# Delta-rule input slabs in pairs by seven block products, inside the gated branch of a hybrid decoder trunk

## The reference

```python
def token_mixer(h, pos0, s_ret, s_gla, s_rwkv, s_shift, p, l):
    proj = (h @ p['w_in'][l]).astype(f32)
    p_ret, p_gla, p_rwkv, p_merge = split_cols(proj, (RET_PROJ, GLA_PROJ, RWKV_PROJ, MERGE_COLS))
    y_ret, sr = retention_branch(p_ret, ...)
    y_gla, sg = gla_branch(p_gla, ...)
    y_rw, sw, ss = rwkv7_branch(p_rwkv, ...)
...
def rwkv7_branch(p_rwkv, S0, prev0, mu, ...):
    prev = jnp.concatenate([prev0[:, None, :], p_rwkv[:, :-1, :]], axis=1)
    xm = p_rwkv + (prev - p_rwkv) * mu
```

## Time and profile before

| | before |
|---|---|
| median of 3 runs | 2505.91 us (2504.74 to 2508.6) |
| the profiled execution | 2506.55 us, span 2504.8 us |
| PE / DVE / ACT / POOL busy | 2448.9 / 1288.9 / 609.0 / 0.2 us |
| TensorE clock, mean of the span | 0.997 of full |
| gated branch, layer 0 | 231 to 384 us of the span |
| gated branch, layer 1 | 1222 to 1376 us of the span |

### The profile page before, as it was taken

The page is one execution under the profiler, slowest core; times in us unless marked ns, Lnnn a source line. Parts: engine busy times, 40 slices in busy tenths (PEclk is TensorE's granted clock), DMA queues, the critical chain, the costliest instruction groups (busy, mean ns, idle before and its releaser), DMA issues. The chain is left out here.

```text
span 2504.8 us, 103575 instructions
## 1 busy us (share of the span) xinstructions
PE 2448.9 (98%) x45930; PEld 2047.9 (82%) x45930; DVE 1288.9 (51%) x3327; ACT 609.0 (24%) x1798; POOL 0.2 (0%) x4
## 2 busy tenths in 40 slices
PE   9999999999999999999999999999999999999998
PEld 8987666666698999898766666679899999888986
DVE  7666666666686676756665666667311111111111
ACT  2233333433311100223333334321111111111111
POOL 0000000000000000000000000000000000000000
PEclk9999999999999999999999999999999999999999
DMA  6334432222243444333443222234899999999997
GB/s 249 111 136 162 150 134 88 83 83 79 90 163 121 159 173 134 133 116 137 154 161 125 84 77 83 83 105 152 321 357 391 385 364 386 393 388 397 407 391 284
DMA packets 146066, 500.42 MB, mean 200 GB/s; under 512 B 18785, under 2 KB 23521, under 8 KB 143361
## 3 DMA queue, kind: packets, MB, share of 16 engines
q1 hardware_dynamic: 145792, 496.44, 54.3%
HBM read 476.08 MB, written 20.29 MB: 198 GB/s over the span
## 5 line engine op out<-in xcount | busy, mean ns | idle before, releaser
L299 PE MATMUL psum<-hT,ring 128*64 128x144 f32 (+1 forms) x4568 | 457.1, 345 | 3.8 <-DVE hT L2419 1.7
L452 PE MATMUL psum<-work,ring 128*64 128x88 f32 (+1 forms) x11264 | 423.8, 235 | 10.3 <-issue 4.3
L452 PEld LDWEIGHTS psum<-work,ring 128*64 128x64 f32 x11264 | 411.6, 136 | 23.4 <-issue 20.5
L299 PEld LDWEIGHTS psum<-hT,ring 128*64 128x64 f32 x4568 | 291.7, 137 | 97.6 <-issue 12.2
L2959 DVE TENSOR_TENSOR work<-psum,work 128x88 f32<-128x88 f32 x176 | 43.9, 249 | 363.5 <-PE psum L452 363.3
L2659 PE MATMUL psum<-work,proj 128*64 128x88 f32 (+1 forms) x5632 | 212.1, 234 | 4.1 <-issue 2.7
L2659 PEld LDWEIGHTS psum<-work,proj 128*64 128x64 f32 x5632 | 205.1, 136 | 10.8 <-issue 9.6
L1765 ACT ACTIVATE work<-psum 128x256 f32<-128x256 f32 (+4 forms) x320 | 104.0, 362 | 349.7 <-PE psum L1676 84.8
L299 PE MATMUL psum<-y_ret,work 128*64 128x144 f32 x2400 | 157.9, 288 | 0.8 <-DVE y_ret L529 0.8
L299 PE MATMUL psum<-work 128*64 128x144 f32 (+4 forms) x2096 | 154.1, 282 | 4.3 <-DVE work L1256 3.6
L299 PEld LDWEIGHTS psum<-y_ret,work 128*64 128x64 f32 x2400 | 150.3, 138 | 1.2 <-issue 1.2
(11 more groups left out here) (514 smaller groups left out, 3725.9 us busy)
## 6 DMA issues: line engine op xcount, KB each, us to landing
ring<-w_ff_dram SPq DMA_DIRECT2D x424, 512.0 KB, 6.9
ring<-w_mix_dram SPq DMA_DIRECT2D x256, 512.0 KB, 4.4
proj<-w_ff_dram SPq DMA_DIRECT2D x128, 512.0 KB, 5.5
proj<-w_ff_dram SPq DMA_DIRECT2D x64, 384.0 KB, 5.7
work<-s_gla_dram SPq DMA_DIRECT2D x8, 1024.0 KB, 5.4
gla_s_out<-work SPq DMA_DIRECT2D x8, 1024.0 KB, 4.7
work<-s_ret_dram SPq DMA_DIRECT2D x8, 512.0 KB, 5.6
ret_s_out<-work SPq DMA_DIRECT2D x8, 512.0 KB, 3.0
```

The costliest lines, as they stand in the source:

```text
L299: last = nc.tensor.matmul(out[64 * c:64 * c + 64], weights[:, 64 * c:64 * c + 64], x, start=start, stop=stop)
L452: mm = nc.tensor.matmul(out[64 * c:64 * c + 64], ring[:, s, k, 64 * c:64 * c + 64], rhs[:, k0 + k, :], start=(k0 + k == 0), stop=(k0 + k = ...
```

## The change

`rwkv`'s 24 input slabs are made in 12 pairs by seven block products, as `retention` does it for the gated branch. PE's generator `row_products` yields 28 steps a pair; a step is two matmuls of 144 columns (4 records). Where `rw(4)` stood, `rw(7)` stands, and `rw(14)` for `rw(8)`, so a pair ends at the end of level 3, at the end of level 7, and at the end of the head. Two of a pair's four weight sums (s1, s3) are made by POOL (`outer_sums`), the other two (s2, s4) by DVE (`inner_sums`). POOL starts pair p when both slabs are there and pair p-2 is done. The sums lie in ring slots 6 and 7 (even pairs), or in `lora_w` and the first two slabs of `merged` (odd pairs); since that would overwrite the input sums, POOL copies those (2304 columns) to `work` once a layer. DVE combines with four instructions a pair (`take_x`, one; `take_y`, two; `take_z`, one), ACT copies one block (`take_first`), and `rw_row` now reads the combined result in SBUF. `new_states` is cut in two around `take_y`; rows and mixes of slabs 4 and 5 of a head move into the next head (behind the last head for head 3).

```diff
+        quad, copied = w(7, HALF), w(4, PAIRS_UP, HALF)
+        first_product = y_gla[:, KT - 1, 0:HALF]
...
+        def row_sums(p):
+            if p % 2 == 0:
+                return list(sum_tiles(ring_wsum, 4, 4))
+            return list(sum_tiles(rest_wsum, 3, 4)) + list(sum_tiles(last_wsum, 1, 4))
+        def fill_bank(p, fill):
+            return B[6 + (p + fill) % 2]
+        def slabs_of_pair(p):
+            return ring[:, 2 * p % 6], ring[:, 2 * p % 6 + 1]
...
+            def row_products():
+                for p in range(PAIRS):
+                    a1, a2 = slabs_of_pair(p)
+                    s1, s2, s3, s4 = row_sums(p)
+                    x, y, z = (fill_bank(p, n) for n in range(3))
+                    kept_sums = copied if p else xsum_kept
+                    xs = [[kept_sums[:, n, k, :] for k in range(PAIRS_UP)] for n in range(4)]
+                    pair_arrived(pe, p)
+                    if p:
+                        pe.wait_ge(sig("y_taken"), p)
+                    for k in range(PAIRS_UP):
+                        in_halves(x[:, 2 * HALF:3 * HALF], a1[:, k], inputs[k][:, 0:HALF], k == 0, k == 3)
+                        yield
...
+                    pe.wait_ge(sig("wsum"), 2 * p + 1)
+                    if p == 1:
+                        pe.wait_ge(sig("copied"), 1)
+                    for k in range(PAIRS_UP):
+                        last = in_halves(x[:, HALF:2 * HALF], s2[:, k], xs[1][k], k == 0, k == 3)
+                        if k == 3:
+                            last.then_inc(sig("first_ps"), 1)
+                        yield
+                    if p:
+                        pe.wait_ge(sig("taken"), p)
+                    pe.wait_ge(sig("outer_sum"), 2 * p + 2)
+                    for k in range(PAIRS_UP):
+                        in_halves(y[:, 0:HALF], s1[:, k], xs[0][k], k == 0, k == 3)
+                        yield
+                    for k in range(PAIRS_UP):
+                        last = in_halves(y[:, HALF:2 * HALF], s3[:, k], xs[2][k], k == 0, k == 3)
+                        if k == 3:
+                            last.then_inc(sig("middle_ps"), 1)
+                        yield
+                    pe.wait_ge(sig("wsum"), 2 * p + 2)
+                    pe.wait_ge(sig("u2"), p + 1)
+                    for k in range(PAIRS_UP):
+                        in_halves(z[:, 0:HALF], s4[:, k], inputs[k + 4][:, HALF:T], k == 0, k == 3)
+                        yield
+                    for k in range(PAIRS_UP):
+                        last = in_halves(z[:, HALF:2 * HALF], a2[:, k + 4], xs[3][k], k == 0, k == 3)
+                        if k == 3:
+                            last.then_inc(slab_done, 2)
+                        yield
+            blocks = row_products()
+            def rw(n):
+                for _ in range(n):
+                    next(blocks, None)
...
-                    rw(4, True)
+                    rw(7)
...
-                rw(4, True)
+                rw(7)
...
-                rw(4, True)
+                rw(7)
...
-                rw(8, True)
+                rw(14)
...
-            pe.wait_ge(sig("row"), GLA_H * 6 + 1)
+            pe.wait_ge(sig("y_taken"), PAIRS)
...
-                act.wait_ge(slab_done, i * 6 + (slabs_before(layer, S_RW) + j + 1))
+                act.wait_ge(sig("taken"), i * 3 + j // 2 + 1)
                 act.wait_ge(sig("mixed"), i * 6 + j + 1)
-                fill_row(row, kept, RW_ORDER[i][j], j % 2, B[6 + j % 2]).then_inc(sig("row"), 1)
+                c = j % 2
+                fill_row(row, kept, RW_ORDER[i][j], c, flat(quad[:, 2 * c:2 * c + 2, :])).then_inc(sig("row"), 1)
+            def take_first(p):
+                act.wait_ge(sig("first_ps"), p + 1)
+                if p:
+                    act.wait_ge(sig("u2"), p)
+                ac(first_product, fill_bank(p, 0)[:, 2 * HALF:3 * HALF], cp).then_inc(sig("first"), 1)
...
-            grant(act, sig("row"), by=2)
...
                 factors(i, 2)
                 decays(i)
                 if i:
+                    rw_row(i - 1, 4)
                     rw_row(i - 1, 5)
                 factors(i, 3)
+                take_first(3 * i)
                 if i:
                     rstd(i - 1)
                 factors(i, 4)
                 take_values(i)
-                rw_row(i, 0)
                 factors(i, 5)
                 take_keys(i)
                 factors(i, 6)
+                rw_row(i, 0)
                 rw_row(i, 1)
                 factors(i, 7)
+                take_first(3 * i + 1)
                 take_middle(i)
-                rw_row(i, 2)
                 if i + 1 < GLA_H:
                     factors(i + 1, 1)
+                rw_row(i, 2)
                 rw_row(i, 3)
                 take_output(i)
-                rw_row(i, 4)
+                take_first(3 * i + 2)
+            rw_row(GLA_H - 1, 4)
             rw_row(GLA_H - 1, 5)
             rstd(GLA_H - 1)
...
+            def outer_sums(p):
+                pair_arrived(pool, p)
+                if p >= 2:
+                    pool.wait_ge(slab_done, slabs_before(layer, S_RW) + 2 * p - 2)
+                s1, s2, s3, s4 = row_sums(p)
+                a1, a2 = slabs_of_pair(p)
+                nc.gpsimd.tensor_tensor(s1, a2[:, 0:4], a2[:, 4:8], ALU.add).then_inc(sig("outer_sum"), 1)
+                nc.gpsimd.tensor_tensor(s3, a1[:, 0:4], a2[:, 0:4], ALU.subtract).then_inc(sig("outer_sum"), 1)
+            pool.wait_ge(retained("y"), RET_H // 2 + 1)
+            outer_sums(0)
+            pool.wait_ge(retained("evac"), 6 + RET_H // 2 * 6)
+            nc.gpsimd.tensor_copy(copied, xsum_kept).then_inc(sig("copied"), 1)
+            for p in range(1, PAIRS):
+                outer_sums(p)
...
-                dve.wait_ge(sig("row"), i * 6 + j + 3)
+                dve.wait_ge(sig("row"), i * 6 + j + 1)
...
+            def inner_sums(p):
+                s1, s2, s3, s4 = row_sums(p)
+                a1, a2 = slabs_of_pair(p)
+                dve.wait_ge(sig("outer_sum"), 2 * p + 2)
+                tt(s2, s1, a1[:, 0:4], ALU.subtract).then_inc(sig("wsum"), 1)
+                dve.wait_ge(sig("wsum"), 2 * p + 1)
+                if p == 1:
+                    dve.wait_ge(sig("copied"), 1)
+                tt(s4, a1[:, 4:8], s2, ALU.subtract).then_inc(sig("wsum"), 1)
...
+            def take_x(p):
+                if p:
+                    dve.wait_ge(sig("row"), 2 * p)
+                dve.wait_ge(sig("first"), p + 1)
+                tt(quad[:, 0:5:4, :], two(fill_bank(p, 0)), rep(first_product, 1, 2), ALU.add).then_inc(sig("u2"), 1)
+            def take_y(p):
+                dve.wait_ge(sig("u2"), p + 1)
+                dve.wait_ge(sig("middle_ps"), p + 1)
+                tt(quad[:, 5:7, :], two(fill_bank(p, 1)), rep(quad[:, 4, :], 1, 2), ALU.add).then_inc(sig("u34"), 1)
+                dve.wait_ge(sig("u34"), p + 1)
+                tt(quad[:, 3, :], fill_bank(p, 1)[:, 0:HALF], quad[:, 6, :], ALU.add).then_inc(sig("y_taken"), 1)
+            def take_z(p):
+                dve.wait_ge(slab_done, slabs_before(layer, S_RW) + 2 * p + 2)
+                tt(quad[:, 1:3, :], two(fill_bank(p, 2)), quad[:, 5:7, :], ALU.add).then_inc(sig("taken"), 1)
...
-                for b in range(NB):
+                for b in sequences:
...
+            inner_sums(0)
             for i in range(GLA_H):
+                p = 3 * i
...
-                    if L == 0 and i:
-                        rw_mix(i - 1, 5)
+                    if L == 0:
+                        if i:
+                            rw_mix(i - 1, 4)
                     if L == 1:
                         scale_keys(i)
-                    if L == 2 and i:
-                        norm(i - 1)
+                        take_x(p)
+                    if L == 2:
+                        if i:
+                            rw_mix(i - 1, 5)
+                            norm(i - 1)
+                        take_y(p)
                     if L == 3:
+                        take_z(p)
+                        inner_sums(p + 1)
+                    if L == 4:
                         rw_mix(i, 0)
                     if L == 5:
+                        take_x(p + 1)
                         rw_mix(i, 1)
                     if L == 6:
                         sequence_keys(i)
+                        take_y(p + 1)
+                    if L == 7:
+                        take_z(p + 1)
+                        inner_sums(p + 2)
                 if i + 1 < GLA_H:
                     distance(i + 1, 1)
                 final_state(i)
@@ -1343,9 +1494,15 @@
                 if i + 1 < GLA_H:
                     level_keys(i + 1, 1)
                     distance_to_end(i + 1)
+                take_x(p + 2)
                 rw_mix(i, 3)
-                new_states(i)
-                rw_mix(i, 4)
+                new_states(i, range(4))
+                take_y(p + 2)
+                new_states(i, range(4, NB))
```

(4 more changed lines are left out.)

21 lines of the change are left out of this document (17 added, 4 removed).

## The result

The changed kernel takes 2544.97 us (median of 4 runs, 2543.62 to 2658.68), the kernel before in the same session 2505.32 us. The ratio is 1.0155, 95% interval 1.0138 to 1.0173: slower by 1.6%, some 39 us.

What follows compares the result with a forecast made beforehand. PE bounded the kernel before; afterwards a DVE loop through `take` of level 7, lengthened by POOL's sums, would. 2506.55 + 7.6 (loop and ends) + 24 (POOL) = 2538 us, 2537 as median; range 2490 to 2562 us.

Steps and rivals of the forecast that it cites:

- the likeliest case: Branch heads: DVE waits for POOL part of the time, 2520 to 2560 us; chance 0.50.
- PE's saving: Products of a head: 336 records, 20.6 us, replace six slabs, 23.6 us; PE saves 3.0 us a head.
- DVE's load: DVE's queue in a head: occupied time goes from 24.8 to 33.4 us, against PE's 33.7.
- The loop: From `take` of level 7 to the next: 6.9 + 0.7 + 28.7 + 1.6 = 37.9 us, 1.2 us more a head.
- the loop alone: Rival for the branch: POOL costs DVE nothing, 2514 us, spanning 2499 to 2516 us; chance 0.24.
- The end of the branch: Shift-row stores to the next phase's first product: two fills, `take_z` and late DVE add 1.8 us a layer.
- The saving of PE behind the last loop: From the last loop's end to the last product: PE saves 0.6 us.
- POOL beside DVE: POOL's sums at pair ends hold up DVE: 3.2 us a head, 2.4 in the first, 24 us for both layers.
- The signs named beforehand: Second head: PE brackets of 3 us or more released by DVE, 39 to 42 us long, longer DVE rows beside POOL.
- its sign of a wrong loop: DVE idle over 2 us a head for anything but `take_x` of the third pair and ACT's exponentials.
- PE stays the bound: Rival for the heads: DVE's loop is under 33.7 us, total 2484 us, half of it 2495 us; chance 0.17.
- Full blocking in every sum: Rival: every POOL sum blocks DVE for its whole length, 7.2 us a head, 58 us, total 2572 us; chance 0.09.

Runs made afterwards that it cites:

- sums early, all queues in line: All four sums on DVE, every queue reordered, first pair's sums ahead of `level_keys`, against the kernel before: 2509.38 us, ratio 1.0015.
- fills: Changed kernel with POOL filling the two sum areas three times each with a constant instead of summing: 2878.66 us, total unusable; second head 37.56 us.
- the kernel with the new order and the shorter mix: All four sums on DVE, PE making 12 steps ahead of `output(i, 0)`, mix cut to two DVE instructions: 2541.42 us, ratio 1.0148 to the kernel before.

## Why the prediction was right

**The time.** 2537 us were predicted, 2545 measured, and the likeliest case, that DVE waits for POOL part of the time, is the one that the runs show.

**PE's saving.** 3.0 us a head were to leave PE with 33.7 us. The best head that was seen (sums early, all queues in line) has PE busy for 34.6 us, so the saving is about 2.1 us. In that head the 336 records of products take 21.6 us, 0.0644 us each, where the step took 0.0613 us from a long row of one kind; PE's other work takes 12.95 us in both kernels. It didn't matter here, since PE wasn't the bound.

**DVE's load.** 33.4 us occupied were predicted. Without POOL's sums the head is 37.55 us with 4.4 us of DVE's waits in it: 33.1 us.

**The loop.** 37.9 us a head were predicted for the loop alone, 37.55 measured; +3.8 us a layer, +3.4 measured (157.2 less 153.8 in layer 0); 2514 us for this rival, 2513.23 measured. The stretch from the `take` of level 7 to `take_x`, 7.6 us predicted (with 0.2 us in it for the hand-over, for which there was no row), is 300.88 - 293.21 = 7.7 us in the run without POOL's sums. DVE's other stands are 2.6 us, 0.9 for ACT's exponentials and 1.7 of mixes for ACT's rows; 0.96 us of them lie inside that stretch and cost nothing, so 1.6 us lie on the loop, as much as predicted, though the wait for rows has the larger part. The loop came out 0.35 us too long because DVE's work on it was put too high, 28.7 us against 37.55 - 7.7 - 1.6 = 28.2.

**The end of the branch.** +1.8 us were predicted from the last square sum to the next phase; it is 6.6 us instead of 5.7, +0.8, with 0.8 us of stand ahead of the square sum, so +1.6 in all. The saving of PE behind the last loop was put at 0.6 us; by the prediction's own figures two slabs less 28 steps are 2 x 3.94 - 6.86 = 1.0 us. The first head without POOL's sums is 37.0 us, 0.8 shorter than before (-1.0 predicted).

**POOL beside DVE** is the term that was mis-sized: 24 us against 31.6. The length of a sum was right (1.27 us and 1.24 from start to start, 1.2 predicted), and so was the reasoning that the two sums behind pair 3i+1 are absorbed, which the run with the moved sums shows by itself. Of the other four I counted two thirds, a share that no row gave; three quarters landed, 3.7 us a head instead of 3.2. Over three loops that is 1.5 us a layer too little. The first head was worse: 41.6 against 37.0 us, 4.6 instead of 2.4. The copy of 2304 columns, priced at nothing because DVE waits there, has a part in it. Without POOL's sums the copy is there too, but it runs from 232.86 to 234.96 us, inside DVE's stand for ACT; POOL's first two sums push it behind that stand. Timeline of the changed kernel, first head:

```profile
234.58 2.11 POOL L1320 COPY work<-merged 128x2304 f32<-128x2304 f32 x1
235.51 1.49 DVE L1357 TENSOR_TENSOR work<-proj,work 128x288 f32<-128x288 f32 x1 [2.05 <-ACT work L1223]
...
236.93 1.51 DVE L1358 TENSOR_TENSOR work<-proj,work 128x288 f32<-128x288 f32 x1
...
238.37 1.75 DVE L1403 TENSOR_TENSOR ring<-ring 128x512 f32<-128x512 f32 x1
...
238.50 1.12 PE L299 MATMUL psum<-work 128*64 128x128 f32 x8 [4.12 <-DVE work L1358]
```

`level_keys` (L1357, L1358) beside that copy and the next POOL sum take 1.49 and 1.51 us instead of 0.45, and PE stands 4.1 us for them. DVE's wait for ACT ended while the copy still ran, and the cover ended with it. From L1357 to the start of the second inner sum DVE needs 4.6 us here and 1.6 without POOL's sums; by the rows, about 1 of these 3 us is the copy and 2 are the sums of the second pair. The other 1.5 us of the first head come with the later pairs.

On the mechanism the Trainium skill, "SBUF — State Buffer", section "Who interferes with whom", says that a DVE instruction with two SBUF inputs contends with a GpSimd instruction that reads SBUF, not with one that only writes it. By that rule, the traces agree in both halves: 0.69 us become 1.58 and 1.65 beside a sum, and stay 0.68 and 0.69 beside fills. The section also calls this an exclusive lock, so that one blocks until the other is done. The traces agree in part: six sums of 1.24 us are 7.4 us a head, and DVE's rows grew by 5.6. Of the difference, 0.8 us are the starts of the three pairs of sums (at 273.64, 290.03 and 302.48 us), when DVE stands or runs rows that read PSUM; the other 1.0 us is open.

**The signs named beforehand.** PE's brackets released by DVE sum to 4.2 us in the second head (at least 3 named), the head is 41.3 us (39 to 42), DVE's waits for PE at `new_states` are gone, DVE's rows beside POOL are longer, and the spacing of POOL's sums is 1.2 us. DVE stands for ACT alone, 1.7 us of it for rows, which the prediction had not named; its sign of a wrong loop was over 2 us.

**What the rivals were worth.** "The loop alone" is what happens without POOL's sums. "PE stays the bound" came near only in the rewritten order (PE busy for 34.6 of 35.9 us), and gave back at the ends what it won. Full blocking in every sum would be 58 us; 31.6 were measured, as DVE's rows grow by 5.6 us a head and not by 7.2, and 1.8 us of these fall into a stand.

## What to carry to other kernels

Before work goes from a full DVE queue to POOL, ask what POOL reads and what DVE runs meanwhile: beside DVE instructions with two SBUF operands a POOL sum cost the kernel 0.66 us, and the same sum on DVE 0.43 us. Count occupied time of an in-order queue, not its busy share of the kernel; DVE at 51% had 11.9 us a head to give, not half of 36.7. And saved PE time is only there if every queue that feeds it is put in a new order with it; each single move gave the gain to the next wait.

## What was not expected of the hardware

The wait of one engine for the other's SBUF reads stands inside its row in the trace, without a bracket: DVE's busy time of 1400.2 us contains it. It shows only when the mean of one form is compared between kernels.

TensorE's clock fell inside the branch, too. Behind PE's 2.49 us stand in the second head of the changed kernel the mean granted clock is 0.60 over the next four microseconds, between the lower of its two levels (1.2 GHz, 0.5) and the full one (2.4 GHz) (windows of all engines; clock, DMA share and GB/s are the last three columns):

```profile
284.00:288.00 4.00, 3.65 (x36) 2.73 (x38) 3.79 (x12) 1.40 (x4) 0.00 (x0) 0.60 0.50 193
288.00:292.00 4.00, 4.00 (x61) 3.63 (x59) 3.75 (x7) 1.07 (x4) 1.97 (x2) 0.97 0.30 73
```

The same products, from that stand to the group behind L1152, take 5.90 us there and 4.35 us without POOL's sums, where the stand was 0.98 us and the clock stayed at 1.00. It cost nothing in this head, as DVE never waits for PE in it: from that stand to `take_x` at 299.08 us DVE stands for ACT alone, at most 0.2 us at a time. Where the others wait for PE it does cost: 1.7 us in the first head of the kernel before with POOL at work. What decides whether the clock falls the runs don't settle: behind stands of 2.1 to 2.7 us at the phase's boundary it fell in some executions and not in others, and in the kernel with the new order and the shorter mix it did not fall behind 2.91 us.
